# Expert weights in 8 KB rows of one matrix per step, norm sums begun early, last expert pair in quarters, output in four parts

## What is computed

```python
def hierarchical_moe(hn, w_router_group, w_router_expert, w_gate, w_up, w_down):
    # top-1 group, then top-2 experts in that group
    ...
    for e in range(N_EXPERTS):                       # 32
        hid = jax.nn.silu(t @ w_gate[e]) * (t @ w_up[e])     # 2048 -> 256
        out = out + (hid @ w_down[e]) * comb[:, e:e + 1]     # 256 -> 2048
# rms_norm(x, g) = x * rsqrt(mean(x * x) + eps) * g, before each part and at the end
```

## Time and profile before

| | us |
|---|---|
| median of 3 runs | 2258.14 |
| lowest and highest run | 2256.07, 2258.84 |
| the profiled execution, device time | 2258.33 |
| its span, first to last instruction | 2256.5 |
| PE busy | 2206.6 (98%) |
| DVE busy | 1315.3 (58%) |
| ACT busy | 914.8 (41%) |
| mean granted TensorE clock | 0.995 |

### The profile page before, as it was taken

One profiled execution on the slowest core, in us unless ns is written; L12 is line 12 of the kernel. 1 busy time (PEld: TensorE's weight loads), 2 busy tenths in 40 slices (PEclk: granted clock), 3 DMA queues, 4 the chain that ended last, 5 costly groups with the idle time before them and its releaser, 6 DMA issues.

```text
span 2256.5 us, 30867 instructions
## 1 busy us (share of the span) xinstructions
PE 2206.6 (98%) x11459; PEld 1675.7 (74%) x11459; DVE 1315.3 (58%) x1757; ACT 914.8 (41%) x1263; POOL 15.7 (1%) x30
## 2 busy tenths in 40 slices
PE   9999999999999999999999999999999999999997
PEld 8886888544444443788888878888888888888886
DVE  7797565322222222766666755767777777764443
ACT  5563454422222221554444544554434343434332
POOL 1000000000000000000000000000000000000000
PEclk9999999999999999999999999999999999999999
DMA  7764455699999999557655455546656656666663
GB/s 256 217 188 139 132 180 190 251 412 413 413 413 412 412 413 408 158 171 226 212 168 169 152 164 186 163 149 194 187 187 189 190 186 187 189 209 194 192 194 120
DMA packets 301181, 518.34 MB, mean 230 GB/s; under 512 B 24032, under 2 KB 196112, under 8 KB 292240
## 3 DMA queue, kind: packets, MB, share of 16 engines
q1 hardware_dynamic: 298272, 505.51, 65.5%
q0 software_dynamic: 2800, 11.34, 1.5%
HBM read 514.63 MB, written 5.27 MB: 230 GB/s over the span
## 4 chain that ended last, share of the span: by engine, by line
PE 85%; DMA 7%; DVE 4%; ACT 2%; issue 1%; SPq 1%; DVEq 0%; ACTq 0%
PE acc L659 30%; PE acc L680 24%; PE acc L683 12%; PE ps L1101 8%; DMA mw<-in_w_expert_up 7%; PE acc L1123 2%; PE tp L1051 2%; DVE wlo L1855 1%; PE tp L768 1%; PE ps L836 1%; PE tp L1063 1%; SPq L448 1%; DMA raw<-in_w_ple_gate 1%; PE ps L1051 1%; PE tp L851 0%
## 5 line engine op out<-in xcount | busy, mean ns | idle before, releaser
L1855 DVE TENSOR_TENSOR wlo<-raw,whi 128x1024 fp32r<-128x1024 f32 x572 | 676.3, 1221 | 221.4 <-ACT whi L1386 217.6
L680 PE MATMUL acc<-xhl,whi 128*128 128x512 f32 x2496 | 790.6, 398 | 1.6 <-DVE wlo L1855 0.7
L1386 ACT ACTIVATE whi<-raw 128x1024 fp32r<-128x1024 f32 x572 | 582.8, 1054 | 364.8 <-DMA raw<-in_w_down 135.3
L683 PEld LDWEIGHTS acc<-xhl,wlo 128*128 128x128 f32 x2496 | 468.9, 188 | 110.8
L683 PE MATMUL acc<-xhl,wlo 128*128 128x256 f32 x2496 | 490.8, 278 | 0.0
L680 PEld LDWEIGHTS acc<-xhl,whi 128*128 128x128 f32 x2496 | 381.5, 189 | 5.8 <-issue 3.0
L1101 PE MATMUL ps<-mw,xg 128*64 128x512 f32 x1024 | 232.2, 597 | 8.8 <-DMA mw<-in_w_expert_up 7.4
L1101 PEld LDWEIGHTS ps<-mw,xg 128*64 128x64 f32 x1024 | 70.0, 137 | 151.3 <-issue 132.6
L659 PE MATMUL acc<-whi,xhl 128*128 128x512 f32 x480 | 157.3, 397 | 0.0
L659 PE MATMUL acc<-whi,ah 128*128 128x512 f32 x336 | 130.7, 389 | 0.0
L659 PE MATMUL acc<-wlo,ah 128*128 128x512 f32 x336 | 130.7, 389 | 0.0
(11 more groups left out here) (405 smaller groups left out, 2456.2 us busy)
## 6 DMA issues: line engine op xcount, KB each, us to landing
raw<-in_w_in SPq DMA_DIRECT2D x352, 256.0 KB, 3.0
raw<-in_w_up SPq DMA_DIRECT2D x352, 256.0 KB, 2.9
mw<-in_w_expert_gate SPq DMA_DIRECT2D x128, 512.0 KB, 9.3
mw<-in_w_expert_up SPq DMA_DIRECT2D x128, 512.0 KB, 10.8
mw<-in_w_expert_down SPq DMA_DIRECT2D x64, 1024.0 KB, 13.0
raw<-in_w_down SPq DMA_DIRECT2D x176, 256.0 KB, 3.4
raw<-in_w_out SPq DMA_DIRECT2D x128, 256.0 KB, 3.3
raw<-in_w_ple_gate SPq DMA_DIRECT2D x64, 256.0 KB, 3.5
```

Source lines behind the costliest of these rows:

```text
L680: pe.matmul(out(ct).rearrange("p (m n) -> p m n", m=2), wh[:, ct * P:ct * P + P], ahl[:, :, k, :], start=first, stop=False, skip_group_che ...
L683: mm = pe.matmul(out(ct)[:, S:2 * S], wl[:, ct * P:ct * P + P], ahl[:, 0, k, :], start=False, stop=last, skip_group_check=True)
L1386: act.activation(whi[:, m % RING, :], raw[:, m % RING, :], ACT.Copy).then_inc(hi_ready, 1)
L1855: dve.tensor_tensor(wlo[:, m % RING, :], raw[:, m % RING, :], whi[:, m % RING, :], ALU.subtract).then_inc(lo_ready, 1)
```

## The change

1. **Experts.** A gate/up step now holds one matrix alone: steps 0 and 1 of a pair the two row halves of gate for both experts, steps 2 and 3 those of up. It is two DMAs of 1 MB with 8 KB in a partition, as down steps were. A gate/up step has 16 matmuls of 256 moving columns in place of 8 of 512.
2. **Router.** The sum of squares is taken over columns 0 to 1535 beside the last mixing block, with the root's table loaded there, and over the last 512 behind it. The late sums stand ahead of the last two `norm_part`. The last transposes come one step earlier. `x_hi` and `embedded` alternate on ACT; DVE writes the first `x_lo` ahead of the ranks' instructions.
3. **Last pair.** It is evicted in quarters of 512 columns, each as soon as its matmuls are done; the two splits come behind the evictions.
4. **The end.** The sum is split in the same way inside the last block of 22 chunks, where DVE also multiplies columns 0 to 1535 by `gfin`. Behind it DVE and ACT scale them (one tile each), and four DMAs write the output.

```diff
@@ loads, SP
-                    load_step(STEPS * g + c, [(w, e, c) for e in (2 * g, 2 * g + 1) for w in (wgp, wup)])
+                    load_step(STEPS * g + c, [((wgp, wup)[c // 2], e, c % 2) for e in (2 * g, 2 * g + 1)])
...
@@ def w_landed(step):
-            return sum(64 if s % STEPS < 4 else 32 for s in range(step % STEP, step + 1, STEP))
+            return 32 * (step // STEP + 1)
...
@@ router, PE
-            before = leading(h, added1, rows=False, made=MADE1, begin=4)
+            before = leading(h, added1, rows=False, made=MADE1, begin=3)
...
@@ def gate_up(g, c):
-                for k in range(4):
+                for k in range(8):
                     for e in range(2):
                         r = slice(64 * e, 64 * e + 64)
-                        x_e = xg[:, g // 2 % 2, 4 * c + k, g % 2 * P + 64 * e:g % 2 * P + 64 * e + 64]
-                        mm = pe.matmul(ps[0][r, :].rearrange("p (a n) -> p a n", a=2), x_e,
-                                       mw[:, s0 + 2 * e:s0 + 2 * e + 2, k * 256:(k + 1) * 256], start=c == 0 and k == 0,
-                                       stop=c == 3 and k == 3, skip_group_check=True)
+                        x_e = xg[:, g // 2 % 2, c % 2 * 8 + k, g % 2 * P + 64 * e:g % 2 * P + 64 * e + 64]
+                        mm = pe.matmul(ps[0][r, c // 2 * 256:c // 2 * 256 + 256], x_e,
+                                       mw[:, s0 + 2 * e + k // 4, k % 4 * 256:(k % 4 + 1) * 256], start=c % 2 == 0 and k == 0,
+                                       stop=c % 2 == 1 and k == 7, skip_group_check=True)
...
@@ def down(g, j):
+                        if g == PAIRS - 1 and j == 1 and (c, b) != (1, 1):
+                            mm.then_inc(y_half, 1)
...
@@ def last_scatter(k):
-                pe.wait_ge(y_ready, 2 * (PAIRS - 1) + (1 if k < 4 else 2))
+                pe.wait_ge(y_ready, 2 * (PAIRS - 1) + (k // 2 + 1 if k < 5 else 4))
...
@@ ACT, new functions
+            def early_rows(junk):
+                act.activation(junk, h[:, 0, 0:1536], ACT.Square, accum_out=ss_parts[:, 0, 0:1]).then_inc(n_early, 1)
+            def late_rows(junk):
+                k = rows.n
+                rows.n += 1
+                act.activation(junk, h[:, 0, 1536:D], ACT.Square, accum_out=ss_parts[:, 1, 0:1]).then_inc(n_ss0, 1)
+                act.wait_ge(n_ss1, k + 1)
+                act.activation(rms[:, :], ss[:, :], ACT.Sqrt, bias=eps[:, 0:1], scale=1.0 / D).then_inc(n_rms, 1)
...
@@ router, ACT
             consume(8 - MADE1)
+            early_rows(junk_ra[:, :])
+            act.activation(warm[:, :], eps[:, :], ACT.Sqrt)
             bl.n += 4
+            h_done()
+            late_rows(hs[:, 0, 1536:D])
             for g in range(MADE1, KT // 2):
                 norm_part(xh, g)
             norms.n += 1
-            h_done()
-            norm_rows(h, hs[:, 0, :])
...
             for t in range(TT):
                 act.activation(x_hi[:, t, :, :], ...).then_inc(xh_ready, 1)
-            embedded(0)
-            embedded(1)
+                embedded(t)
...
@@ last pair, ACT (DVE alike)
+            def evict_last():
+                for k in range(4):
+                    if k < 3:
+                        act.wait_ge(y_half, k + 1)
+                    else:
+                        act.wait_ge(w_used, STEPS * PAIRS)
+                    act.activation(yh[:, k * 512:(k + 1) * 512], acc[k // 2][:, k % 2 * 512:k % 2 * 512 + 512], ACT.Copy,
+                                   scale=w_slot[:, PAIRS - 1:PAIRS]).then_inc(y_hi, 1)
...
+            evict_last()
             split(0)
             split(1)
-            evict(PAIRS - 1)
...
@@ DVE, new functions
+            def late_rows(junk, early):
+                own(dve.tensor_tensor_reduce(junk, h[:, 1, 1536:D], h[:, 1, 1536:D], 1.0, 0.0, ALU.mult, ALU.add,
+                                             ss_parts[:, 1, 1:2]))
+                mine()
+                dve.wait_ge(n_early, early)
+                dve.wait_ge(n_ss0, k + 1)
+                dve.tensor_tensor(ss[:, :], ss_parts[:, 0, :], ss_parts[:, 1, :], ALU.add).then_inc(n_ss1, 1)
+                dve.wait_ge(n_rms, k + 1)
+                dve.reciprocal(rstd2[:, k % 2, :], rms[:, :]).then_inc(n_inv, 1)
...
@@ router, DVE
+            low_rows(0)
             dve.wait_ge(rank_mm, 1)
...
             slot_columns(0, 8)
             mine()
             dve.sem_inc(slots_ready, 1)
-            for t in range(TT):
-                dve.wait_ge(xh_ready, t + 1)
-                dve.scalar_tensor_tensor(x_lo[:, t, :, :], ...)
+            low_rows(1)
...
@@ the end, DVE, in the last block of 22 chunks
+                    early_rows(junk_f[:, 1, :])
+                    consume(4)
+                    dve.wait_ge(gf_in, 16)
+                    dve.wait_ge(n_early, 2)
+                    weighted(0)
+                    consume(4)
+                    mine()
+                    weighted(1)
...
-            norm_rows(h, hs[:, 1, :], spread=False)
+            late_rows(junk_f[:, 1, 0:512], 2)
...
+            dve.tensor_scalar(h[:, 0, 0:1536], h[:, 0, 0:1536], rstd(0), None, ALU.mult).then_inc(fin_ready, 1)
             for t in range(TT):
-                dve.scalar_tensor_tensor(h[:, t, :], h[:, t, :], rstd2[...], gfin[:, :], ALU.mult, ALU.mult)
+                dve.scalar_tensor_tensor(h[:, t, 1536:D], h[:, t, 1536:D], rstd(t), gfin[:, 1536:D], ALU.mult, ALU.mult)
...
@@ the end, ACT
+            act.activation(h[:, 1, 0:1536], h[:, 1, 0:1536], ACT.Copy, scale=rstd2[:, (rows.n - 1) % 2, 1:2])
...
@@ the end, SP: four DMAs, tile 0 columns 0:1536, tile 0 1536:2048, tile 1 0:1536, tile 1 1536:2048, each behind its own wait
```

More of the change, by code:

```diff
@@ L520, in _ @@
             assert n.n == N_CHUNKS
[L521 to L524 removed]
+            sp.wait_ge(fin_ready, 1)
+            sp.dma_start(out[0, 0:P, 0:1536], h[:, 0, 0:1536]).then_inc(out_done, 16)
+            sp.wait_ge(fin_ready, 2)
+            sp.dma_start(out[0, 0:P, 1536:D], h[:, 0, 1536:D]).then_inc(out_done, 16)
+            sp.wait_ge(fin_scaled, 1)
+            sp.dma_start(out[0, P:2 * P, 0:1536], h[:, 1, 0:1536]).then_inc(out_done, 16)
+            sp.wait_ge(fin_ready, 3)
+            sp.dma_start(out[0, P:2 * P, 1536:D], h[:, 1, 1536:D]).then_inc(out_done, 16)
+            sp.wait_ge(out_done, 64)
         @block.gpsimd
@@ L1620, in embedded @@
                 consume(1)
-            embedded(0)
-            embedded(1)
+            act.wait_ge(n_inv, rows.n)
+            for t in range(TT):
+                act.activation(x_hi[:, t, :, :], h[:, t, :].rearrange("p (q k) -> p k q", k=KT), ACT.Copy,
+                               scale=rstd2[:, 1, t:t + 1]).then_inc(xh_ready, 1)
+                embedded(t)
             act.wait_ge(rt_read, 2)
@@ L1832, in _ @@
             for b in range(4):
-                consume(FF_T // 2)
+                if b < 3:
+                    consume(FF_T // 2)
+                else:
+                    consume(4)
+                    act.wait_ge(acc_free[(bl.n - 1) % 2], (bl.n - 1) // 2 + 1)
+                    early_rows(junk_f[:, 0, :])
+                    act.activation(warm[:, :], eps[:, :], ACT.Sqrt)
+                    consume(FF_T // 2 - 4)
                 bl.n += 1
@@ L1837, in _ @@
             h_done()
-            norm_rows(h, hs[:, 0, :])
+            late_rows(junk_f[:, 0, 0:512])
+            act.wait_ge(n_inv, rows.n)
+            act.activation(h[:, 1, 0:1536], h[:, 1, 0:1536], ACT.Copy,
+                           scale=rstd2[:, (rows.n - 1) % 2, 1:2]).then_inc(fin_scaled, 1)
         @block.vector
@@ L1888, in norm_rows, with early_rows @@
                     dve.sem_inc(n_diag, 1)
+            def early_rows(junk):
+                own(dve.tensor_tensor_reduce(junk, h[:, 1, 0:1536], h[:, 1, 0:1536], 1.0, 0.0, ALU.mult, ALU.add,
+                                             ss_parts[:, 0, 1:2]))
+            def late_rows(junk, early):
+                k = rows.n
+                rows.n += 1
+                own(dve.tensor_tensor_reduce(junk, h[:, 1, 1536:D], h[:, 1, 1536:D], 1.0, 0.0, ALU.mult, ALU.add,
[6 more added lines that the diff above has]
+                dve.reciprocal(rstd2[:, k % 2, :], rms[:, :]).then_inc(n_inv, 1)
             def take_rows():
@@ L2260, in _ @@
                     consume(8 - MADE1)
+                    early_rows(junk_rv[:, :])
                 if b == 1:
@@ L2331, in slot_columns, with low_rows @@
                                           iota[:, :].unsqueeze(1).to_broadcast(like), ALU.is_equal))
+            def low_rows(t):
+                dve.wait_ge(xh_ready, t + 1)
+                dve.scalar_tensor_tensor(x_lo[:, t, :, :], h[:, t, :].rearrange("p (q k) -> p k q", k=KT), rstd2[:, 1, t:t + 1],
+                                         x_hi[:, t, :, :], ALU.mult, ALU.subtract).then_inc(xl_ready, 1)
+            low_rows(0)
             dve.wait_ge(rank_mm, 1)
@@ L2451, in _, with evict_last @@
                 moved(g, 3)
```

(23 more changed lines are left out.)

25 lines of the change are left out of this document (14 added, 11 removed).

## The result

The changed kernel takes 2243.95 us (median of 4 runs, 2243.14 to 2244.48); the kernel before took 2258.43 in the same comparison. The ratio is 0.994, with a 95% interval of 0.9928 to 0.9952: 14.5 us less. The profiled execution took 2244.48 us, its span is 2242.7, where before it was 2256.5.

A forecast was written before the change was run, and what follows sets the result against it. DMA was taken to bound the expert stage, PE only 0.56 us a pair behind. Terms -7.0 - 3.3 - 0.2 - 3.4 = -13.9 took the profiled 2258.3 us to 2244.4, median about 2244.3, range 2239 to 2251.

The forecast's parts named there:

- Experts, -7.0: Expert stage: 8 KB pieces shorten the weights' stream, and the stage ends 7.0 us sooner; bounds -9 and +1.
- 60 x 0.18 = 10.8 us: Expert stage: 60 gate/up steps load in 4.96 us instead of 5.14, lowering the DMA's floor by 10.8 us.
- PE's cost of 0.02 us a step: Expert stage: allowance for twice the matmuls at half the width, 1.3 us in all.
- the two floors: Expert stage: the DMA's floor falls 10.8 us and PE's 7.8; the later one ends the stage.
- PE's floor (-7.8): Expert stage: PE's own time falls 5.6 us over pairs 4 to 13 and 3.5 in the last, with 1.3 back.
- The other sign: Expert stage, profile after: 420 GB/s or more in all stretches, DMA share below 1.02 here and there.
- Router, -3.3: Before the experts: earlier logits and reordered DVE work start the first gather at 405.1 instead of 408.46; bounds -1.7 and -3.8.
- Last pair, -0.2: Behind the last pair: yl is ready earlier, but PE's branch still delays the scatter; 0.2 us gained, bounds 0 and -2.4.
- The end, -3.4: After the last matmul: shorter late sum, earlier table load and four output DMAs save 3.4 us; bounds -2.4 and -4.0.
- A: Rival, expert stage: 8 KB brings nothing for gate and up, stage falls 0 to 1 us, total 2250.7; chance 0.14.
- B: Rival: PE starts behind the last pair without the branch's delay, floors hardly disturb each other (-9), total 2239.8; chance 0.14.
- C: Rival, expert stage: weight loads no longer hide, PE becomes the bound, +39 us or 2297; chance 0.04.

The follow-up runs named there:

- short body: Changed kernel with 8 of the 144 matmuls behind PE's branch left and the rest of that work left out: 2241.56 us, ratio 0.9931.
- the experts alone: Kernel before with only the expert weights' part of the change (8 KB pieces, one matrix a step, 256-column matmuls): 2252.18 us, ratio 0.9973.
- the early branch: Changed kernel with PE's branch taken behind the first step of the last pair, nothing left out: 2248.25 us, ratio 0.9956.
- the branch in pieces: Changed kernel with PE's branch cut into ten and DVE's two splits behind the last pair's first four sums, nothing left out: 2246.48 us, ratio 0.9955.

## Why the prediction was right

It forecast 2244.3 us with 2239 to 2251, and the median is 2243.95. The mechanism of three parts held; that of the experts was in part wrong, and its sum came near by some luck. Term by term:

- **Experts, -7.0, came out as -7.3,** from terms that were partly mis-sized. The step was "60 x 0.18 = 10.8 us" for the stream. The landing interval of a gate/up step fell from 5.12 to 4.97 in the median, 0.15 and not 0.18: the stretch of 4 KB pieces in the earlier trace rows held an interval of 5.47. The stream behind step 9 has 56 such steps and fell by 6.8, 0.12 a step. The runs with 4 KB pieces in the new shape explain most of the rest: that shape alone makes the stream 1.1 us longer. The estimate from the Trainium skill (DMA: Bandwidth & Descriptors, "Why small descriptors are slow") that stands in the prediction was 1.2%; measured are (5.11 - 4.97) / 5.11 = 2.7%, less than the 3.7% of the rows and over twice the estimate.
- PE's cost of 0.02 us a step is right: four steps a pair, 29.97 became 30.05. But I added the two floors up wrongly. I took PE's floor (-7.8) as the later one and then disturbed it a little. The stream ends the stage; PE sets the pace of the pairs while the ring has a lead and no more. Here lies the luck: the stream's term was put 4 us too high, and it did no harm only because the sum went by PE's. That PE shows no wait for weights in most pairs held, and it did not mean what I took it for. The other sign, 420 GB/s or more in all stretches, did not come: 416 to 420.
- **Router, -3.3, measured -3.06.** `lg` moved by 1.48 where I had 1.7; the gather came 0.3 behind the 405.1 expected, less than two executions of the changed kernel differ by (405.40 and 404.72), and the shift was still 3.0 us at step 9's issue.
- **Last pair, -0.2, measured +0.18.** The point that mattered was that the quarters bring nothing while the branch holds PE, and it did: 3.93 us (forecast 3.7). What held it, left open then, is now known: the jump over a body not yet fetched. With a short body the branch takes 0.21 us and PE doesn't stop; that it is a fetch is read from the packet that goes with every long one, 2.5 us before its end. The runs also show why the splits' new place cost nothing: they lay in the branch's time. Without the branch they cost 1.6.
- **The end, -3.4, measured -3.43.** The first output DMA starts 2.62 us behind the late sum (forecast 2.6), and the output has landed at 2242.28, 9.24 behind it (9.2).
- **Rivals.** A fell (all 8 KB pieces are faster, those of gate and up too). B's branch did not end earlier with this change; what it would have brought there, 2.4, is borne out by the 2.8 without the branch. C fell: 137 ns a load under slots of 0.22.

## What to carry to other kernels

Where a stream of DMAs bounds a stage, look at the size of the contiguous piece per partition before the number or the size of the DMAs: here 8 KB instead of 4 KB was worth 2.7% of a step's time, and with 4 KB pieces two DMAs of 1 MB did as well as four of 512 KB (495.1 and 495.4 us). But keep all 128 partitions in each DMA. An engine that shows no wait can still be off the path: read who waits in the last steps of the stage, after the buffer's lead is used up. And before work is made ready earlier for an engine, check that the engine itself can start: a forward jump over a long body cost PE 3.9 us here, and it is to be seen as a sequencer row of that line, not as a wait.

## What the runs showed of the hardware

- A forward jump on PE over 8 matmuls took 0.20 to 0.33 us, over 80 matmuls 5.3 us, over 144 matmuls 5.9 to 6.3; in the last two a packet of 16 KB on the instruction queue starts 0.7 to 2.7 us behind PE's last matmul and the branch ends 2.5 us after it, in all eleven traces that have one (893.49 and 896.00 in the changed kernel). A loop's jump back over 256 matmuls took 0.21 us, without a packet. The Trainium skill (Runtime: NRT & Kernel Launch, "Instruction fetch mechanics") says that a taken branch whose target is outside the window already fetched forces a DMA fetch before execution goes on. The traces agree: a packet goes with each of the slow branches and with none of the fast ones.
- Instructions are traffic too. The change gives PE 2048 more records (1024 matmuls and their loads), and the profile's page counts 81 packets on the instruction queue where it had 73. Each takes 1.0 to 1.1 us of one DMA engine. That these delay the weights, and are the 1.1 us that the new shape costs the stream, fits but was not tested alone.
- DMAs of 64 partitions with 8 KB pieces moved 266 GB/s at a DMA share of 1.01, those of 128 partitions 419.
- PE's stop costs twice: with it the granted clock fell from 2.4 to its lower level, 1.2 GHz. In the changed kernel PE stood for 3.93 us and the clock was down for 3.4 (897.42 to 900.83). It was down for 6.8 us in three runs: the experts alone (stop of 3.46), the early branch (4.84; a step took 6.03 us in place of 3.67) and the branch in pieces (5.42). Without the branch, and with the short body, PE did not stop there, and the clock stayed at 2.4 GHz from 441 to 2231 us.
